# Rotations, turns, gates and norms spread between units, and MLA's four short projections interleaved with a longer one

## The chip, the cores and the metric

The kernel runs on one core of a Trainium2 chip, with inputs, weights and output in HBM. The metric is device time in microseconds of one execution. The engines of the core are TensorE (PE; its weight loads are PEld), VectorE (DVE), ScalarE (ACT), GpSimd (POOL) and SyncE (SP, which issues the DMAs); each runs its own program, and semaphores order them.

## The reference, cut to what matters

256 tokens of width 1024 in float32 go through two layers of a first block and two of a second.

```python
# first block, per layer (h = rms_norm(x))
cq, ckv, k_rope, mq, mk, mv, rq, rk, rv, rg, g_mla, g_moba, g_ret = split(h @ w_in)
q  = rms_norm(cq) @ w_q_up;  kv = rms_norm(ckv) @ w_kv_up        # MLA's short projections
o_mla  = causal_attention(q, [kv_nope, rope(k_rope)], v)          # 8 heads, rope on 32 of 96
o_moba = causal attention of partial_rope(mq), partial_rope(mk), mv   # 8 heads of 64
o_ret  = silu(rg) * group_norm(retention(rope(rq), rope(rk), rv))     # 4 heads, decay in place of softmax
merged = sum(sigmoid(g_i) * (o_i @ w_branch_i));  x = x + merged @ w_out
x = x + square(relu(rms_norm(x) @ w_mlp_up)) @ w_mlp_down
# second block, per layer (u = rms_norm(h))
gq, gk, gv, gg, ra_f, ra_b, aq, ak, av, gate_a, gate_b = split(u @ w_in)
branch_a = (rms_norm(gla(gq, gk, gv, decays)) * silu(gg)) @ w_o_gla
branch_b = gqa(axial_rope(rms_norm(aq)), axial_rope(rms_norm(ak)), av) @ w_o_attn   # 8 heads of 128
h = h + rms_norm((sigmoid(gate_a) * branch_a + sigmoid(gate_b) * branch_b) @ w_out)
# then a gated MLP and a gated embedding
```

## The kernel before, in words

Every weight matrix is cut into chunks of at most 512 columns, and a chunk into *units* of two blocks of 128 rows. `Plan` lists the 600 units in the order in which every engine goes through them (`units_first`: 140 in each first layer, `units_second`: 160 in each second one; numbers below count within a layer). For a unit SyncE loads 128x1024 floats into one of four `raw` slots; ScalarE copies them to `hi`, rounded (L1015); VectorE takes `lo` = `raw` - `hi` (L1396; GpSimd for some of the MLP's units); TensorE makes twelve products (L556): two row tiles, two blocks, and hi x hi, lo x hi, hi x lo. The short `kv_up` chunks have one block, six products. A chunk accumulates in one of two pairs of PSUM banks, `acc`; pairs alternate from chunk to chunk, and a chunk's first product waits until the earlier chunk of its pair is drained (`pair0_drained`, `pair1_drained`).

`Stream.to(n)` and `Stream.on(n)` go to unit n of the layer, or n units on. Everything else is written by hand between such calls, and each engine's own list of calls sets where in its queue a piece stands. ScalarE is three units ahead with `hi`, VectorE two with `lo`, and both read out a finished chunk one unit later (`after` and `read_out`, EVAC = 1). So VectorE's queue has the low part of unit v + 3 ahead of the read-out of a chunk that ended at unit v.

The order in a first layer: `w_in` chunks in units 0 to 11 (latents, MQ, MK), `q_up` in 12 and 13, `kv_up` in 14 and 15, MV 16 to 19, RQ with RK 20 to 23, RV 24 to 27, RG (`silu`) 28 to 31, the gates 32 to 55, then the branches. VectorE rotates MoBA's rows at 13 and MLA's q at 17 (`rope_heads`, six instructions of L1526 to L1531). At 19 TensorE transposes ("turns") MLA's q and k into the four `mix` banks (L523); ScalarE copies q to `qT`, VectorE k to `kT` (L1414); TensorE waits for these (`emptied`) and starts the heads. A head is: scores on TensorE (L585, L627), shift on VectorE (L1546, L1549), exponential on ScalarE (L1104), a turn (L604), a copy to `probT` by ScalarE (L1029), the context (L616). `MLA_UNITS`, `RET_UNITS` and `MOBA_UNITS` say how many units stand in each step. In a step with scores these stand between the turn and the context that needs its copy; in MoBA only even steps have them. Retention follows MLA and MoBA follows retention, each with turns and copies at its opening. Group norm and gating of retention's output (`retention_out`, five steps) lie beside MoBA's heads.

In a second layer (`second_layer`) the four heads of gated linear attention stand at units 30 to 41; beside them VectorE makes the squares and rotations of the grouped attention's q and k (`head_squares`, `head_rope`). At 46 these are turned, after `rows_ready`; from 48 on come its eight heads, two units each, with exponentials at L1275 and copies to `attnT` at L1029, waited for at L824. The gate chunks are units 40 to 55, read out with Sigmoid at L1123. Where ScalarE changes between functions of different tables, it runs an ACT_TABLE_LOAD first.

Of the kernel before, what the change touches and what calls it, by code (L numbers as in the profile page):

```python
# [129 lines left out]

def units_first(ln):
# [16 lines left out]
    return (woven(p[0], p[1]) + straight(p[2], *q_up, *kv_up, *p[3:])  # L148
# [4 lines left out]
def units_second(ln):  # L153
# [30 lines left out]
    'bank0_filled'        : [103, 0, 0],  # L184
    'bank1_filled'        : [106, 0, 0],
    'bank2_filled'        : [106, 0, 0],
    'bank3_filled'        : [86, 0, 0],
    'bank0_drained'       : [103, 0, 0],
    'bank1_drained'       : [106, 0, 0],
    'bank2_drained'       : [106, 0, 0],  # L190
    'bank3_drained'       : [86, 0, 0],
    'pair0_drained'       : [73, 0, 0],
    'pair1_drained'       : [73, 0, 0],
# [3 lines left out]
    'rows_ready'          : [66, 0, 0],  # L197
# [8 lines left out]
    'gates_ready'         : [2, 0, 0],  # L206
    'glu_ready'           : [18, 0, 0],
# [26 lines left out]
class Plan:  # L234


    def __init__(self):
# [262 lines left out]
def tensor_program(nc, pe, n, L):  # L500
# [120 lines left out]
    def softmax_heads(tag, heads, q, k, v, units):  # L621
        blocks = {(1, 0): 0, (1, 1): P, (0, 0): TOK}
        for h in range(heads + 2):
# [5 lines left out]
            if h >= 2:  # L629
                emptied((tag, "t", h - 2))  # L630
# [12 lines left out]
    def first_layer():  # L643
# [9 lines left out]
        s.to(19)  # L653
# [10 lines left out]
        pe.wait_ge(*n.next("rows_ready"))  # L664
        for w, col in (("q", RQ), ("k", RK)):
            turn(("ret", w, 0), lambda t, k: L.proj[:, t, col + k * P:col + (k + 1) * P], (0, 1))
        turn_half("mla", 0, y_tile)
        emptied(("ret", "q", 0)); emptied(("ret", "k", 0))
        for h in range(RET_H + 1):
# [5 lines left out]
            s.on(RET_UNITS[h])  # L675
            if h:
# [4 lines left out]
        for w, col in (("q", MQ), ("k", MK)):  # L681
            for j in range(2):
                turn(("moba", w, j), lambda t, k: L.proj[:, t, col + k * P:col + (k + 1) * P], (2 * j, 2 * j + 1))
# [6 lines left out]
        s.to(50)  # L690
        pe.wait_ge(*n.next("rows_ready", 2))
        turn_half("moba", 0, y_tile)
        s.to(55)
# [26 lines left out]
    def second_layer():  # L720
# [90 lines left out]
        for h in range(AQ_H + 2):  # L811
            if h < AQ_H:
                kv = h // (AQ_H // AKV_H)
                fill(("gqa", "s", h), lambda b: [nc.tensor.matmul(L.mix[:, b, t * TOK:(t + 1) * TOK], L.qT[:, h, t * P:(t + 1) * P],  # L814
                                                                 L.kT[:, kv, :], **f32) for t in range(NT)], (0, 1, 2))
            if h >= 2:
# [20 lines left out]
            s.on(2 if 1 <= h <= 8 else 0)  # L837
# [164 lines left out]
Q_SCALE, VAR_G, ROOT_G = 232, 96, 136  # L1002
# [3 lines left out]
def scalar_program(nc, act, n, L, io):  # L1006
# [144 lines left out]
    def sigmoids(*cols):  # L1151

        for c in L.plan.chunks:
            if c.ln == ln and c.name == "gate" and any(g <= c.to < g + D for g in cols):
                act.wait_ge(*n.at(f"pair{c.pair}_drained", c.turn + 1))
        for g in cols:
            last = nc.scalar.activation(L.proj[:, :, g:g + D], L.proj[:, :, g:g + D], ACT.Sigmoid)
        last.then_inc(*n.up("gates_ready"))
# [16 lines left out]
    def first_layer():  # L1175
# [7 lines left out]
        s.to(19)  # L1183
        for j in range(4):
            empty(("mla", "q", j), L.qT[0:QK_D, 2 * j:2 * j + 2, :], 2 * TOK, QK_D)
# [941 lines left out]
```

## Time and profile before

| | |
|---|---|
| median of 3 runs | 1988.53 us (1987.27 to 1989.32) |
| the profiled execution's own time | 1988.42 us |
| its span, first to last instruction | 1986.3 us |
| TensorE products | 96% of the span |
| VectorE; ScalarE; GpSimd | 63%; 50%; 6% |
| mean granted TensorE clock | 0.988 |
| `lo` (L1396), x552 | 1226 ns each |
| `hi` (L1015), x600 | 1060 ns each |

The profile is of one execution. An engine is busy from the start to the end of an instruction; idle time is told with what ended it. TensorE's clock is the granted share of its full speed of 2.4 GHz. A product of 512 columns is recorded with some 390 ns, but the next begins earlier, since they are pipelined.

### The profile page before, as it was taken

The numbers are of one execution on the slowest core, as the hardware profiler recorded it, in microseconds if no ns is written. First come the engines' busy times: TensorE is split into PE (matmuls) and PEld (weight loads), VectorE is DVE, ScalarE is ACT, GpSimd is POOL, SyncE is SP. The second block draws the span as 40 slices with busy tenths as digits, with TensorE's granted clock in tenths as the row PEclk, the third lists the DMA queues.
The fourth block names the chain that finished last, engine by engine and source line by source line (L and its number), as shares of the span: only waits on it lengthen the run. The fifth ranks groups of instructions, "written<-read, shape, count | busy, mean of one in ns | idle before, by whom it ended". The sixth has DMA issues, their size and how long they took to land.

```text
span 1986.3 us, 25019 instructions
## 1 busy us (share of the span) xinstructions
PE 1906.1 (96%) x9121; PEld 1550.8 (78%) x9121; DVE 1254.4 (63%) x2095; ACT 995.4 (50%) x1516; POOL 127.9 (6%) x52
## 2 busy tenths in 40 slices
PE   7899999999999999999999999999989999999997
PEld 6777788888777788877777887888767777878885
DVE  6756674546756574545768657666675695676656
ACT  4445554444445554444653746545456347464544
POOL 0000008300000007500000000000000000000000
PEclk9999999999999999999999999999989999999999
DMA  6444555565534556555543444656544344455562
GB/s 225 136 125 130 167 172 180 183 186 180 159 106 123 176 162 195 169 174 155 189 131 122 128 159 148 196 160 205 171 123 162 122 128 128 149 176 184 169 204 93
DMA packets 167500, 315.33 MB, mean 159 GB/s; under 512 B 12282, under 2 KB 20172, under 8 KB 167252
## 3 DMA queue, kind: packets, MB, share of 16 engines
q1 hardware_dynamic: 166784, 312.01, 50.6%
q8 instruction: 74, 1.21, 0.2%
q10 hardware_dynamic: 596, 1.73, 0.2%
q14 instruction: 46, 0.38, 0.1%
HBM read 312.65 MB, written 1.05 MB: 158 GB/s over the span
## 4 chain that ended last, share of the span: by engine, by line
PE 85%; DVE 8%; ACT 4%; issue 2%; DMA 0%; ACTq 0%; DVEq 0%
PE acc L556 73%; PE mix L523 4%; DVE lo L1396 2%; PE mix L616 2%; ACT hi L1015 1%; PE mix L824 1%; PE mix L795 1%; PE mix L585 1%; PE mix L814 1%; PE mix L782 1%; PE mix L604 1%; ACT junk L1090 0%; DVE kT L1414 0%; PE mix L754 0%; DVE x L1496 0%
## 5 line engine op out<-in xcount | busy, mean ns | idle before, releaser
L1015 ACT ACTIVATE hi<-raw 128x1024 fp32r<-128x1024 f32 x600 | 633.2, 1060 | 599.6 <-PE acc L556 546.9
L1396 DVE TENSOR_TENSOR lo<-raw,hi 128x1024 fp32r<-128x1024 f32 x552 | 665.6, 1226 | 217.4 <-ACT hi L1015 201.7
L556 PE MATMUL acc<-hi,xTh 128*128 128x512 f32 (+3 forms) x1760 | 696.6, 396 | 24.2 <-DVE lo L1396 14.6
L556 PE MATMUL acc<-hi,xTl 128*128 128x512 f32 (+3 forms) x1760 | 680.1, 386 | 0.0
L556 PE MATMUL acc<-lo,xTh 128*128 128x512 f32 (+3 forms) x1760 | 679.3, 386 | 0.0
L556 PEld LDWEIGHTS acc<-hi,xTh 128*128 128x128 f32 x1760 | 335.0, 190 | 106.6 <-issue 39.8
L556 PEld LDWEIGHTS acc<-hi,xTl 128*128 128x128 f32 x1760 | 334.3, 190 | 66.8
L556 PEld LDWEIGHTS acc<-lo,xTh 128*128 128x128 f32 x1760 | 335.4, 191 | 59.8
L987 POOL TENSOR_TENSOR lo<-raw,hi 128x1024 fp32r<-128x1024 f32 x48 | 127.7, 2687 | 694.5 <-ACT hi L1015 694.5
L556 PE MATMUL acc<-hi,hTh 128*128 128x512 f32 x432 | 172.0, 398 | 0.3 <-DVE lo L1396 0.3
L556 PE MATMUL acc<-hi,hTl 128*128 128x512 f32 x432 | 171.2, 396 | 0.0
L556 PE MATMUL acc<-lo,hTh 128*128 128x512 f32 x432 | 171.2, 396 | 0.0
L1424 DVE TENSOR_TENSOR hTl<-mix,hTh 128x256 fp32r<-128x256 f32 x108 | 38.4, 418 | 119.1 <-ACT hTh L1037 119.1
L556 PEld LDWEIGHTS acc<-hi,hTh 128*128 128x128 f32 x432 | 81.4, 188 | 20.0 <-issue 0.7
L556 PEld LDWEIGHTS acc<-hi,hTl 128*128 128x128 f32 x432 | 81.4, 188 | 19.8
L556 PEld LDWEIGHTS acc<-lo,hTh 128*128 128x128 f32 x432 | 81.4, 188 | 19.3
L1037 ACT ACTIVATE hTh<-mix 128x256 fp32r<-128x256 f32 x108 | 32.9, 390 | 54.0 <-PE mix L523 54.0
L556 PE MATMUL acc<-hi,oTh 128*128 128x512 f32 (+1 forms) x136 | 54.5, 401 | 5.1 <-DVE y L1582 5.1
L556 PE MATMUL acc<-lo,oTh 128*128 128x512 f32 (+1 forms) x136 | 53.6, 394 | 0.0
L556 PE MATMUL acc<-hi,oTl 128*128 128x512 f32 (+1 forms) x136 | 53.5, 393 | 0.0
L1104 ACT ACTIVATE prob<-prob,small 128x256 f32<-128x256 f32 x64 | 28.7, 449 | 49.3 <-DVE small L1549 49.3
L523 PE MATMUL mix<-const,y 128*128 128x128 f32 (+1 forms) x360 | 48.2, 279 | 0.0
(222 smaller groups left out, 1614.3 us busy)
## 6 DMA issues: line engine op xcount, KB each, us to landing
raw<-in_w_in SPq DMA_DIRECT2D x200, 512.0 KB, 3.8
raw<-in_w_ffn_in SPq DMA_DIRECT2D x80, 512.0 KB, 4.3
raw<-in_w_mlp_up SPq DMA_DIRECT2D x64, 512.0 KB, 3.8
raw<-in_w_mlp_down SPq DMA_DIRECT2D x64, 512.0 KB, 4.5
raw<-in_w_ffn_out SPq DMA_DIRECT2D x44, 512.0 KB, 4.3
raw<-in_w_out SPq DMA_DIRECT2D x32, 512.0 KB, 4.1
raw<-in_w_o_gla SPq DMA_DIRECT2D x16, 512.0 KB, 3.7
raw<-in_w_o_attn SPq DMA_DIRECT2D x16, 512.0 KB, 3.7
```

Source lines behind the costliest of these rows:

```text
L523: yield nc.tensor.transpose(L.mix[0:width, b, i * TOK + t * P:i * TOK + (t + 1) * P], rows(t, k), L.ident)
L556: last = nc.tensor.matmul(out, a[:, t * P:(t + 1) * P], w[:, slot, part, 0:c.n], start=(k == 0 and a is ah and w is L.hi), stop=(k == c.k_ ...
L585: yield nc.tensor.matmul(L.mix[:, b, c:c + w], q[:, a:a + P], k[:, 0:w], start=True, stop=True)
L604: yield nc.tensor.transpose(L.mix[:, b, i * P:(i + 1) * P], L.prob[:, h % 2, i * P:(i + 1) * P], L.ident)
L616: last = nc.tensor.matmul(L.mix[:, b, (t * per + i) * dv:(t * per + i + 1) * dv], L.probT[:, h % 2, c:c + P], v(kt, h), start=(kt == 0), s ...
L782: last = nc.tensor.matmul(L.mix[:, b, m * GLA_V:(m + 1) * GLA_V], L.ks[r, d, c // 2, h * P:(h + 1) * P], gv(r, c // 2), **f32)
L987: nc.gpsimd.tensor_tensor(L.lo[:, slot], L.raw[:, slot], L.hi[:, slot].bitcast(F32), ALU.subtract).then_inc(*n.up("low_by_pool"))
L1015: nc.scalar.activation(L.hi[:, slot], L.raw[:, slot], ACT.Copy).then_inc(*n.up("hi_ready"))
L1037: last = nc.scalar.activation(dst, L.mix[:, b, i * TOK:(i + 1) * TOK], ACT.Copy if gain is None else ACT.Identity, scale=scale)
L1104: last = nc.scalar.activation(p, p, ACT.Exp, bias=L.small[:, SHIFT + 2 * s + 1 - t:SHIFT + 2 * s + 2 - t], scale=scale, accum_out=L.small[ ...
L1396: v.tensor_tensor(L.lo[:, slot], L.raw[:, slot], L.hi[:, slot].bitcast(F32), ALU.subtract).then_inc(*n.up("low_by_dve"))
L1424: last = v.tensor_tensor(lo, src, hi.bitcast(F32), ALU.subtract)
```

## The change

Short projections: `between` puts one unit of MV behind each of the four, and a chunk's pair is now the other one than that of the unit before. Turns of MLA, retention and MoBA: one unit (`BEHIND_TURNS`) between the turns and the wait for their copies; retention's turns go ahead of MLA's last context, MLA's output is turned inside retention, three of MoBA's four turns stand ahead of retention's last context; steps have other numbers of units. VectorE's MoBA rotation moves to head 1 of MLA, `retention_out` a step later and its last step to unit 54. RG is drained by Identity, and one Silu in place does the gate at 51; the sigmoids stand apart. In the second layers low parts go between the halves of the rotations, the group norm's roots move into the heads (`gla_roots`), gates are drained by Identity with two late sigmoids, and the last heads have a unit ahead of each context.

```diff
+def between(short, c):
+
+    return [(a, 0) if i == 0 else (c, j) for j, a in enumerate(short) for i in range(2)]
...
-    return (woven(p[0], p[1]) + straight(p[2], *q_up, *kv_up, *p[3:])
+    return (woven(p[0], p[1]) + straight(p[2]) + between([*q_up, *kv_up], p[3]) + straight(*p[4:])
...
-                c.pair = len(self.chunks) % 2
+                c.pair = 1 - self.unit[u - 1][0].pair if u else 0
...
-MLA_UNITS = [2, 2, 2, 1, 2, 2, 1, 2, 1, 0]
-RET_UNITS = [0, 1, 1, 1, 1]
-MOBA_UNITS = [2, 1, 1, 1, 2, 1, 1, 1, 1, 0]
+MLA_START, BEHIND_TURNS = 21, 1
+MLA_UNITS = [1, 2, 2, 1, 2, 1, 1, 2, 1, 0]
+RET_UNITS = [0, 1, 1, 1, 0]
+MOBA_UNITS = [1, 1, 1, 1, 2, 1, 1, 1, 1, 0]
```

TensorE, first layers (`softmax_heads` and `first_layer`):

```diff
             if h >= 2:
+                if h == heads + 1 and ahead_of_last:
+                    ahead_of_last()
                 emptied((tag, "t", h - 2))
...
-        s.to(19)
+        s.to(MLA_START)
         pe.wait_ge(*n.next("rows_ready"))
...
+        s.on(BEHIND_TURNS)
         for j in range(4):
             emptied(("mla", "q", j)); emptied(("mla", "k", j))
+        def turn_ret():
+            pe.wait_ge(*n.next("rows_ready"))
+            for w, col in (("q", RQ), ("k", RK)):
+                turn(("ret", w, 0), lambda t, k: L.proj[:, t, col + k * P:col + (k + 1) * P], (0, 1), among=(0, 1, 2))
+
         softmax_heads("mla", MLA_H, lambda h: L.qT[0:QK_D, h, :], lambda h: L.kT[0:QK_D, h, :],
-                      lambda t, h: L.vm[:, t, h, :], MLA_UNITS)
...
+                      lambda t, h: L.vm[:, t, h, :], MLA_UNITS, turn_ret)
+
+        s.on(BEHIND_TURNS)
         emptied(("ret", "q", 0)); emptied(("ret", "k", 0))
...
             s.on(RET_UNITS[h])
+            if h == 2:
+                pe.wait_ge(*n.next("rows_ready"))
+                turn_half("mla", 0, y_tile, (0, 1, 2))
+            if h == RET_H:
+                for w, col, j in (("q", MQ, 0), ("q", MQ, 1), ("k", MK, 0)):
+                    turn(("moba", w, j), lambda t, k: L.proj[:, t, col + k * P:col + (k + 1) * P], (2 * j, 2 * j + 1), among=(0, 1, 2))
...
+        turn(("moba", "k", 1), lambda t, k: L.proj[:, t, MK + k * P:MK + (k + 1) * P], (2, 3), among=(0, 1, 2))
+        s.on(BEHIND_TURNS)
```

TensorE, second layers:

```diff
+            if h >= AQ_H:
+                s.on(1)
             if h >= 2:
...
-            s.on(2 if 1 <= h <= 8 else 0)
+            s.on(2 if 1 <= h < AQ_H else h == AQ_H)
```

ScalarE:

```diff
-        if c.name == "gate":
+        if c.name == "gate" or c.name == "silu" and ln < LAYERS:
...
-                                            ACT.Identity if ln < LAYERS and c.to < G_MOBA else ACT.Sigmoid if ln >= LAYERS or c.to < G_RET else ACT.Identity,
+                                            ACT.Sigmoid if c.name == "gate" and ln < LAYERS and G_MOBA <= c.to < G_RET else ACT.Identity,
...
+    def silu_of_retention():
+
+        c = next(c for c in L.plan.chunks if c.ln == ln and c.name == "silu")
+        act.wait_ge(*n.at(f"pair{c.pair}_drained", c.turn + 1))
+        nc.scalar.activation(L.proj[:, :, RG:RG + COLS], L.proj[:, :, RG:RG + COLS], ACT.Silu).then_inc(*n.up("silu_ready"))
...
-        s.to(50)
+        s.to(51)
+        silu_of_retention()
+        s.to(52)
         split_half("moba", 0)
-        sigmoids(G_MLA, G_RET)
+        s.to(53)
+        sigmoids(G_MLA)
         s.to(55)
+        sigmoids(G_RET)
+        s.to(57)
         split_half("ret", 0)
...
+            if h == AQ_H - 1:
+                s.on(1)
+                sigmoids(at2(G_A))
+                s.on(1)
...
+        s.to(67)
+        sigmoids(at2(G_B))
```

VectorE, first layers:

```diff
-        s.to(13)
-        rope_heads(proj[:, :, MQ:MV].rearrange("p t (h d) -> p t h d", d=MOBA_D), 2 * MOBA_H, MOBA_R // 2, "moba")
-        s.to(17)
+        s.to(18)
         rope_heads(y[:, :, 0:MLA_H * QK_D].rearrange("p t (h d) -> p t h d", d=QK_D)[:, :, :, NOPE:], MLA_H, ROPE // 2, "mla")
+        s.to(20)
         tell("rows_ready")
...
+            if h == 1:
+                rope_heads(proj[:, :, MQ:MV].rearrange("p t (h d) -> p t h d", d=MOBA_D), 2 * MOBA_H, MOBA_R // 2, "moba")
+            elif h == 3:
                 rope_heads(proj[:, :, RQ:RV].rearrange("p t (h d) -> p t h d", d=RET_K), 2 * RET_H, RET_K // 2, "ret")
-
+                tell("rows_ready")
...
-        softmax_heads("moba", MOBA_H, MOBA_D ** -0.5, 0, MOBA_UNITS, lambda h: retention_out(h) if h < 5 else None)
+        softmax_heads("moba", MOBA_H, MOBA_D ** -0.5, 0, MOBA_UNITS, lambda h: retention_out(h - 1) if 1 <= h < 5 else None)
...
+        s.to(54)
+        retention_out(4)
```

VectorE, second layers:

```diff
-            elif h == 2:
-                for t in range(NT):
-                    head_rope(0, 4, t)
-            elif h == 3:
-                head_squares(4, 8)
-                for t in range(NT):
-                    head_rope(4, 8, t)
-            s.on(3)
+            if h in (1, 3):
+                head_squares(2 * h - 2, 2 * h + 2)
+            s.on(1)
+            if h >= 2:
+                head_rope(4 * h - 8, 4 * h - 4, 0)
+            s.on(1)
+            if h >= 2:
+                head_rope(4 * h - 8, 4 * h - 4, 1)
+            s.on(1)
         head_squares(8, 10)
         s.on(1)
         head_roots()
         s.on(1)
-        for t in range(NT):
-            head_rope(8, 10, t)
+        scale_keys()
+        head_rope(8, 10, 0)
+        s.on(1)
+        head_rope(8, 10, 1)
         tell("params_free")
         tell("tmp_free")
         tell("rows_ready")
...
-            if h < 2:
-                gla_out(h)
...
+            if h == 0:
+                gla_roots()
+            elif h < AQ_H:
+                s.on(1)
+                if h <= 2:
+                    gla_out(h - 1)
+                s.on(1)
```

`gla_roots` holds the group norm's instructions that stood at `s.to(45)`, unchanged.

## Rows read from the trace of the kernel before

**Rows 1.** The page, busy time of each engine.

```profile
PE 1906.1 (96%) x9121; PEld 1550.8 (78%) x9121; DVE 1254.4 (63%) x2095; ACT 995.4 (50%) x1516; POOL 127.9 (6%) x52
```

**Rows 2.** Waits of TensorE (in total, times, longest, us).

```profile
PE acc L556 <- DVE lo L1396: 14.9, 22, 2.0
...
PE mix L616 <- ACT probT L1029: 9.2, 14, 1.1
...
PE mix L824 <- ACT attnT L1029: 7.1, 6, 2.2
```

**Rows 3.** Windows: us, busy by engine (instructions), PE clock, DMA.

```profile
73.27:76.68 3.41, 3.41 (x10) 2.64 (x9) 2.44 (x7) 1.93 (x5) 0.00 (x0) 0.50 0.18 17
...
440.00:460.00 20.00, 20.00 (x87) 16.10 (x86) 8.90 (x8) 7.43 (x7) 0.00 (x0) 1.00 0.64 189
...
588.68:592.09 3.41, 3.41 (x10) 2.63 (x9) 1.94 (x3) 0.00 (x0) 0.00 (x0) 0.50 0.13 15
```

**Rows 4.** Timeline of TensorE, first layers: start, us; idle before in brackets.

```profile
46.62 0.39 PE L556 MATMUL acc<-hi,oTh 128*128 128x512 f32 x1
...
53.36 0.51 PE L556 MATMUL acc<-hi,oTh 128*128 128x512 f32 x1 [2.37 <-DVE y L1582]
...
55.41 0.50 PE L556 MATMUL acc<-hi,oTh 128*128 128x512 f32 x1 [0.37 <-DVE y L1582]
...
58.24 0.50 PE L556 MATMUL acc<-hi,xTh 128*128 128x512 f32 x1 [1.17 <-DVE vm L1582]
...
72.03 0.89 PE L585 MATMUL mix<-kT,qT 96*128 96x256 f32 x4 [1.83 <-DVE kT L1414]
...
126.03 0.88 PE L616 MATMUL mix<-vm,probT 128*128 128x64 f32 x6 [1.12 <-ACT probT L1029]
...
130.64 0.88 PE L616 MATMUL mix<-vm,probT 128*128 128x64 f32 x6 [0.58 <-ACT probT L1029]
...
132.60 1.09 PE L523 MATMUL mix<-const,proj 128*128 128x128 f32 x8 [1.08 <-DVEq L1388]
...
151.24 1.97 PE L523 MATMUL mix<-const,proj 128*128 128x128 f32 x16 [0.79 <-DVE y L1746]
...
154.65 0.92 PE L627 MATMUL mix<-kT,qT 64*128 64x256 f32 x8 [1.45 <-DVE kT L1414]
...
587.35 0.92 PE L673 MATMUL mix<-qT,kT 64*128 64x256 f32 x8 [2.04 <-DVE oTl L1424]
```

**Rows 5.** Timeline of VectorE at the short projections.

```profile
48.37 0.42 DVE L1526 TENSOR_TENSOR tmp<-proj,const 128x256 f32<-128x256 f32 x1
...
56.53 0.87 DVE L1582 TENSOR_SCALAR km<-acc,small 128x256 f32<-128x256 f32 x2
...
57.32 0.87 DVE L1582 TENSOR_SCALAR vm<-acc,small 128x256 f32<-128x256 f32 x2
...
61.05 0.42 DVE L1526 TENSOR_TENSOR tmp<-y,const 128x256 f32<-128x256 f32 x1
```

**Rows 6.** ScalarE by line and form (xcount, busy us, mean ns, idle before).

```profile
L1157 ACT ACTIVATE proj<-proj 128x2048 f32<-128x2048 f32 x4 | 7.4, 1906 | 0.0
```

**Rows 7.** Window of a second layer, columns as in rows 3.

```profile
1066.12:1092.18 26.06, 24.07 (x113) 18.22 (x113) 24.32 (x80) 9.54 (x14) 0.00 (x0) 1.00 0.45 140
```

**Rows 8.** Timeline of all engines, the same second layer.

```profile
1078.48 0.47 PE L556 MATMUL acc<-hi,xTh 128*128 128x512 f32 x1 [1.99 <-DVE lo L1396]
...
1091.52 0.28 DVE L1531 TENSOR_TENSOR proj<-proj,tmp 128x128 f32<-128x128 f32 x1
...
1092.18 2.35 PE L523 MATMUL mix<-const,proj 128*128 128x128 f32 x20
...
1093.36 0.17 DVE L1951 TENSOR_SCALAR small<-small 128x8 f32<-128x8 f32 x1
...
1106.74 1.28 ACT L1123 ACT_TABLE_LOAD   x1
...
1110.79 1.56 PE L824 MATMUL mix<-proj,attnT 128*128 128x128 f32 x6 [2.16 <-ACT attnT L1029]
```

More of the change, by code:

```diff
@@ L196 @@
     'scaled_rows'         : [4, 0, 0],
-    'rows_ready'          : [66, 0, 0],
+    'rows_ready'          : [68, 0, 0],
     'ple_rows'            : [8, 0, 0],
@@ L619, in context, with softmax_heads @@
             last.then_inc(*n.up(f"bank{b}_filled"))
-    def softmax_heads(tag, heads, q, k, v, units):
+    def softmax_heads(tag, heads, q, k, v, units, ahead_of_last=None):
         blocks = {(1, 0): 0, (1, 1): P, (0, 0): TOK}
@@ L689, in first_layer @@
                       lambda t, h: L.proj[:, t, MV + h * MOBA_D:MV + (h + 1) * MOBA_D], MOBA_UNITS)
-        s.to(50)
-        pe.wait_ge(*n.next("rows_ready", 2))
+        s.to(52)
+        pe.wait_ge(*n.next("rows_ready"))
         turn_half("moba", 0, y_tile)
-        s.to(55)
+        s.to(57)
+        pe.wait_ge(*n.next("rows_ready"))
         turn_half("ret", 0, lambda t, k: L.y[:, t, COLS + k * P:COLS + (k + 1) * P])
@@ L1149, in embedded, with sigmoids @@
         nc.scalar.activation(L.embed[:, :, c.to:c.to + COLS], pair(c), ACT.Copy).then_inc(*n.up(f"pair{c.pair}_drained"))
-    def sigmoids(*cols):
+    def sigmoids(g):
         for c in L.plan.chunks:
-            if c.ln == ln and c.name == "gate" and any(g <= c.to < g + D for g in cols):
+            if c.ln == ln and c.name == "gate" and g <= c.to < g + D:
                 act.wait_ge(*n.at(f"pair{c.pair}_drained", c.turn + 1))
-        for g in cols:
-            last = nc.scalar.activation(L.proj[:, :, g:g + D], L.proj[:, :, g:g + D], ACT.Sigmoid)
-        last.then_inc(*n.up("gates_ready"))
+        nc.scalar.activation(L.proj[:, :, g:g + D], L.proj[:, :, g:g + D], ACT.Sigmoid).then_inc(*n.up("gates_ready"))
+    def silu_of_retention():
+        c = next(c for c in L.plan.chunks if c.ln == ln and c.name == "silu")
+        act.wait_ge(*n.at(f"pair{c.pair}_drained", c.turn + 1))
+        nc.scalar.activation(L.proj[:, :, RG:RG + COLS], L.proj[:, :, RG:RG + COLS], ACT.Silu).then_inc(*n.up("silu_ready"))
     def hidden(c):
@@ L1585, in read_out @@
     def read_out(c):
-        if c.name in ("gate", "plain", "ple") or c.name == "normed" and (c.weight == "w_out_2" or c.to):
+        if c.name in ("gate", "plain", "ple") or c.name == "silu" and ln < LAYERS or c.name == "normed" and (c.weight == "w_out_2" or c.to):
             return
@@ L1600, in read_out @@
         elif c.name.startswith("branch"):
-            if c.name == "branch_mla" and c.to == 0:
+            if c.name != "branch_moba" and c.to == 0:
                 dve.wait_ge(*n.next("gates_ready"))
@@ L1604, in read_out @@
                  "branch_gla": at2(G_A), "branch_attn": at2(G_B)}[c.name] + c.to
-            if c.name not in ("branch_mla", "branch_ret"):
+            if c.name == "branch_moba":
                 gate = L.plan.chunk(ln, "gate", g)
@@ L1677, in retention_out @@
         elif step == 4:
+            dve.wait_ge(*n.next("silu_ready"))
             link(v.tensor_tensor(o, o, proj[:, :, RG:RG + COLS], ALU.mult))
@@ L1829, in head_rope, with gla_roots @@
         rope(r[:, :, :, 0, :], r[:, :, :, 1, :], c, sn, [end - first, 2, A_D // 4], L.tmp, c_b=c_b, s_b=s_b)
+    def gla_roots():
+        dve.wait_ge(*n.next("squared", NT * GLA_H))
+        link(v.tensor_scalar(col(VAR_G, 8), col(VAR_G, 8), NORM_EPS, None, ALU.add))
+        inverse_root(VAR_G, ROOT_G, 8)
+        b, use = L.banks.get((ln, "gla", "o", GLA_H - 1))
+        dve.wait_ge(*n.at(f"bank{b}_drained", use + 1))
     def gla_out(g):
@@ L1948, in second_layer @@
         tell("rows_ready")
-        s.to(45)
-        dve.wait_ge(*n.next("squared", NT * GLA_H))
-        link(v.tensor_scalar(col(VAR_G, 8), col(VAR_G, 8), NORM_EPS, None, ALU.add))
-        inverse_root(VAR_G, ROOT_G, 8)
-        b, use = L.banks.get((ln, "gla", "o", GLA_H - 1))
-        dve.wait_ge(*n.at(f"bank{b}_drained", use + 1))
         s.to(46)
@@ L1982, in second_layer @@
                 split_half("attn", 0)
-            s.on(2 if 1 <= h <= 8 else 0)
+            if h == 0:
+                gla_roots()
+            elif h < AQ_H:
+                s.on(1)
+                if h <= 2:
+                    gla_out(h - 1)
+                s.on(1)
+            elif h == AQ_H:
+                s.on(1)
         s.to(66)
```

69 lines of the change are left out of this document (37 added, 32 removed).

## The prediction

> **What bounds the kernel now.** I read the page first: TensorE is busy 1906.1 of 1986.3 us [rows 1], so no edit to another engine is worth more than the 80.2 us in which TensorE stands idle, plus what its clock loses. The waits of TensorE come next [rows 2]: the reader is to see that they are many and short, 22 on VectorE's low parts, 14 on a transposed probability block, and none longer than 2.5 us but two at the start of the kernel and of a block. Then the windows by stage [rows 3]: a plain stretch makes 87 matmuls in 20 us, 0.23 us each, 2.76 us for a unit of twelve, with VectorE and ScalarE under half busy. So in the long stages nothing can be won, and the change leaves them alone. The same view has stretches of 3.41 us at a granted clock of 0.50, that is the 1.2 GHz level in place of 2.4, each worth 1.7 us. I find five of them in the stages touched: at 73.3, 506.8, 588.7, 1110.9 and 1643.4; two stand in the rows. Each began within 1.4 us after a TensorE wait of 1.8 to 2.4 us. But of nine such waits in these stages (53.4, 72.0, 505.7, 524.4, 587.4, 1078.5, 1110.8, 1610.9, 1643.3) four had no such stretch behind them. Last, TensorE's timeline gives the place and size of each wait [rows 4].
>
> **The change, part by part.** The sum is made against the profiled execution, 1988.42 us, which is its span of 1986.3 and 2.1 around it; the median of the runs, 1988.53, is the same to 0.1 us.
>
> *Short projections, first layers.* Now the four follow one another, and each needs the accumulator pair of the last but one. The MoBA rotation (six VectorE instructions of 0.42 us, 2.4 in all) and the low parts stand before the read-outs, and TensorE waits 2.37, 0.37 and 1.17 us in layer 0 [rows 4], 2.37 and 0.10 in layer 1. After: all four use one pair, with a unit of MV between. TensorE, from the first matmul at 46.62: q_up 2.8, MV 2.75, second q_up (256 columns, an estimate of half a unit) 1.45, MV 2.75, kv_up (six matmuls) 1.4, MV 2.8, kv_up 1.4, MV 2.8, which is 64.8. VectorE: the read-outs of the two q_up come in time (51.0 against 52.2; 55.6 against 56.4). Then the low part of unit 19 can't begin before unit 15 is done (56.4) and ScalarE's copy of 1.06 has followed, so it ends at 58.9; first kv_up read-out 0.87 + 0.79 [rows 5], 60.6, just in time; the q rotation, moved in front of `s.to(20)`, 2.36 (0.42 each, at 61.05 and five more), 63.0; two low parts, 65.3; second kv_up read-out 1.66, 67.0. Unit 20 needs that pair and stands ready at 64.8: a new wait of 2.15 us. So the wait that takes the place of the old ones is VectorE's second kv_up read-out. The unit added behind the turns covers the copies to kT: 1.83 goes. Layer 0: 2.37 + 0.37 + 1.17 + 1.83 - 2.15 = 3.6, with the slow stretch at 73.3 (1.7) 5.3. Layer 1: 2.37 + 0.10 + 1.83 - 2.15 = 2.15, with that at 506.8 3.85. The DMAs of the short weights are issued one unit apart in place of back to back, in the same queue and number; I cost them at nothing, because no TensorE wait here ends on a transfer. MoBA's rotation goes to head 1 of MLA: there VectorE has two units, 5.5 us, for two low parts, a shift, a read-out and the 2.4 us, 7.1 us in all, but its low parts run two units ahead, so 1.6 us late is inside the slack of one unit. Uncovered it would cost that 1.6 us a layer.
>
> *Heads' end, retention, MoBA's opening.* At the end of MLA TensorE waits 1.12 (a table load and a sigmoid read-out stand ahead of the block's copy), 0.58 (no scores cover the last head's copy) and 1.08 (`rows_ready`, told only after the heads) [rows 4]. After, the silu chunk is drained by Identity with no load, and 1.12 becomes the 0.58 that all heads without scores have: 0.54 won. Retention's turns stand ahead of the last head's context and cover 0.58; `rows_ready` is told at head 3, 1.08 won. At MoBA's opening 0.79 and 1.45 go: bank 3 isn't used for turns any more, and a unit stands behind them. Layer 1 alone also has 2.04 for the low parts of MLA's output [rows 4], and the slow stretch at 588.7 behind it; the turn moves a stage later, with a unit behind. 0.54 + 0.58 + 1.08 + 0.79 + 1.45 = 4.44 per layer; 2.04 + 1.7 more in layer 1. The added wait on `rows_ready` before MLA's half has retention's contexts queued behind it, but three units lie since its signal. The five waits of 0.58 in MoBA stay, since odd heads still have no scores ahead.
>
> *Silu.* The trace has no Silu. Its bounds are the Copy of the same tile, 1.06 us, and the Sigmoid of a tile twice as wide, 1.91, plus one table load, 1.28, or none [rows 6, 8]; I take 1.06 with a load ahead of it and one more at the sigmoids behind it. With these, and the two sigmoids of 1.91 put apart, ScalarE's high part of unit 56 ends 13.9 us after unit 50 began and VectorE's low part at 15.1, where TensorE wants it at 17.3: 2.2 us to spare, 1.3 with the longer instruction. So nothing is on the path at either end; uncovered, the load and the instruction would cost 2.3 us a layer. VectorE loses two multiplications per layer, off the path.
>
> *Second layers.* VectorE is the bound from 1066.12 to 1092.18: 24.32 us busy of 26.06 [rows 7], the rest being the gaps between dependent instructions. TensorE waits 1.99 at 1078.48, then reaches the turns of gqa at 1092.18, right when the last rotation is done (1091.52 + 0.28, signals 0.3) [rows 8]. The change puts a low part between the halves of each rotation, and the wait of 1.99 goes. But VectorE's work before `rows_ready` is not less: it gains one low part (unit 46's), 1.15 us, and the group norm's roots, moved back, stood behind `rows_ready` anyway. So it ends at 1093.2, and TensorE, now earlier, waits there about 2.9 us and 1.1 before, at unit 43. The turns come 1.05 us later than before: a loss. In the heads, the 2.16 at 1110.79 is ScalarE's chain to the first attnT copy: table load 1.28, read-out, copy [rows 8]. The load goes; but the roots (twelve instructions, 0.2 apart from 1093.36 on, 2.43 in all [rows 8]) stand between the two shifts where gla_out(0) stood with four of 0.42, 1.67: 1.28 - 0.76 = 0.5 is won, with the slow stretch of 1.7 behind it. Of the six waits on attnT [rows 2] the other four are (7.1 - 2 x 2.16) / 4 = 0.69 each, two a layer, at the last heads, and are covered by units: 1.38. Two more switches between kinds of matmul cost 0.12 each. Layer: 0.5 + 1.7 + 1.38 - 1.05 - 0.24 = 2.3. Deferred sigmoids are two instructions of 1.91 on ScalarE, which copies high parts three units ahead (5.9 us of slack against 3.2): nothing.
>
> The Trainium skill ("ScalarE: Activation LUTs", section "What ACT_TABLE_LOAD costs") gives 1283 ns for the load and a drain of some 1380 ns more. Here the load at 1106.74 takes 1.28 us and the activation behind it begins at 1108.04, so this trace shows no drain. By the page the sum would be 1.4 us larger in each second layer, 2.8 in all.
>
> *Sum.* 5.3 + 4.4 in layer 0, 3.85 + 4.4 + 3.7 in layer 1, 2 x 2.3: 26.3 us with no new slow stretch. New waits of 2.15 (twice) and 2.9 (twice) are of the size of which five in nine were followed by one; I count two, 3.4 us. Won: 22.9. 1988.4 - 22.9 = 1965.5.
>
> **Rivals.**
> *Every cover holds.* If VectorE catches up at unit 20 and before gqa, neither new wait appears: 26.3 + 2 x 2.15 + 2 x (1.05 + 1.99) = 36.7, 1951.7. For it: VectorE is idle half the time elsewhere. Against: the chain above has no slack from 58.9 on. Chance 0.15.
> *The clock.* Slow stretches behind all four new waits and both of those at attnT that stay (1.6 us): 26.3 - 6 x 1.7 = 16.1, 1972.3. For it: five in nine. Chance 0.17.
> *The covers do less than they say.* The waits at the ends of stages are VectorE's and ScalarE's backlog, not the delay of one copy, and come back behind the next unit: then 2 x 4.44 + 2.04 are not won, 15.4 less 3.4, 1976.4. For it: 151.24 and 154.65 stand in a row. Against: what ends most of them is one copy that was issued as soon as its turn was done [rows 4]. Chance 0.10.
> *Slower: the heads fall behind.* MLA's heads get 13 units in place of 15, MoBA's 10 in place of 11. If a head's chain (shift, exponential, transpose, copy) no longer fits behind a single unit, TensorE waits at each head, at 1.12 us as at 126.03: 32 heads, 35.8 us, 1965.5 + 35.8 = 2001.3. It decides from 0.72 us a head. Against: single-unit heads with scores ahead show no wait at all, all 14 of [rows 2] are at heads without. Chance 0.05.
> The forecast itself has 0.53, with 1959 to 1971.
>
> **How the numbers follow.** The range reaches from between the first rival and the forecast to the third: 1953 to 1977. About 0.2 % is what this measurement can tell from no change. Faster than that 0.92, same 0.03, slower 0.05.
>
> **What would show it.** Right: no TensorE wait at the kv_up units, one of 2 us before unit 20 that ends on VectorE's vm; no wait at the first scores of MLA, retention and MoBA; one of 2 to 3 us at gqa's turns that ends on VectorE's rotation; attnT's first wait near 1.6; no ACT_TABLE_LOAD at the read-out line of the gates. Wrong: waits of 0.6 to 1.1 us at heads that have scores ahead, or more than two slow stretches in these stages.

## The result, and the profile after

The changed kernel takes 1964.83 us (median of 4 runs, 1963.9 to 1965.03) where the kernel before, on the same chip, takes 1987.99 (4 runs, 1987.27 to 1989.32): ratio 0.9877, 95% interval 0.9865 to 0.9889. The forecast was 1965.5 in a range of 1953 to 1977, and "faster" had a chance of 0.92. The profiled execution took 1965.03 us, span 1963.1, which is 23.2 less than before.

Busy time by engine on the page, to be held against [rows 1]: TensorE's busy time fell by 3.4 us, its idle time by 19.8.

```profile
PE 1902.7 (97%) x9121; PEld 1550.2 (79%) x9121; DVE 1251.3 (64%) x2091; ACT 987.7 (50%) x1510; POOL 127.9 (7%) x52
```

TensorE's waits (in total, times, longest), to be held against [rows 2]. Low parts fell from 14.9 to 11.4 us, transposed blocks from 14 to 12, attnT from six to two. Two lines have other waits under them than before: vm has the second kv_up read-out in both first layers (before, one wait of 1.17), and the turns' wait on VectorE's signal (DVEq) is now at gqa's turns, 2.5 each, where before it was at retention's, 1.1 each.

```profile
PE acc L563 <- DVE lo L1437: 11.4, 19, 1.6
...
PE mix L623 <- ACT probT L1049: 7.0, 12, 0.6
PE mix L530 <- DVEq L1429: 4.9, 2, 2.5
...
PE acc L563 <- DVE vm L1623: 3.9, 2, 2.0
PE mix L844 <- ACT attnT L1049: 2.7, 2, 1.3
```

TensorE's timeline (start, us; idle before in brackets), answering to [rows 4] and to the rows of TensorE in [rows 8]. A row without brackets began without a wait: so do the first scores of MLA (L592), retention (L685) and MoBA (L634), where before 1.83, 2.04 (layer 1) and 1.45 stood.

```profile
67.61 0.50 PE L563 MATMUL acc<-hi,xTh 128*128 128x512 f32 x1 [1.95 <-DVE vm L1623]
...
78.35 0.82 PE L592 MATMUL mix<-kT,qT 96*128 96x256 f32 x4
...
124.68 0.88 PE L623 MATMUL mix<-vm,probT 128*128 128x64 f32 x6 [0.58 <-ACT probT L1049]
...
132.94 0.92 PE L685 MATMUL mix<-qT,kT 64*128 64x256 f32 x8
...
151.36 0.92 PE L634 MATMUL mix<-kT,qT 64*128 64x256 f32 x8
...
510.20 0.50 PE L563 MATMUL acc<-hi,xTh 128*128 128x512 f32 x1 [1.95 <-DVE vm L1623]
...
1091.78 1.16 PE L844 MATMUL mix<-proj,attnT 128*128 128x128 f32 x8 [1.34 <-ACT attnT L1049]
...
1604.35 0.89 PE L530 MATMUL mix<-const,proj 128*128 128x128 f32 x6 [2.45 <-DVEq L1429]
```

Windows (columns as in [rows 3]) of four of the ten stretches at a granted clock of 0.50, the 1.2 GHz level: the first and last are the only ones in stages that the change touches, the other two stand in layer 2's opening (its first units, up to gated linear attention), which it doesn't touch.

```profile
69.07:72.49 3.41, 3.41 (x11) 2.62 (x10) 1.25 (x2) 0.00 (x0) 0.00 (x0) 0.50 0.61 181
929.23:936.06 6.83, 5.21 (x14) 4.17 (x15) 5.75 (x10) 2.12 (x2) 0.00 (x0) 0.50 0.77 250
963.37:966.78 3.41, 3.41 (x10) 2.64 (x9) 3.19 (x3) 0.91 (x1) 0.00 (x0) 0.50 0.32 124
1605.07:1608.48 3.41, 3.41 (x18) 3.32 (x17) 0.83 (x2) 2.84 (x5) 0.00 (x0) 0.50 0.62 184
```

**Where the time went.** I took the start of the same unit's first matmul in both traces, at both ends of each stage touched. In layer 0 the unit before the short projections starts 0.69 us later than before, the second unit of MLA's branch 9.21 earlier: 9.9 won. Likewise layer 1, from 9.09 to 22.57 earlier: 13.5; layer 2, from 19.05 to 22.54: 3.5; layer 3, from 21.17 to 23.07: 1.9. That is 28.8 in all. Outside, 5.6 were lost: 0.7 in the first 44 us, 3.5 in the opening of layer 2, 1.4 in that of layer 3. Where times of a stage are compared below, they are taken in the same way.

### The profile page after: what moved, and what is told of

Its sections match the earlier page's. It is cut to its first block, busy times and chain, and to the rows that moved or that the text cites. A ratio compares the mean times of both kernels' runs of the same rounds, so it can differ in the third digit from the quotient of the medians.

```text
span 1963.1 us, 25017 instructions
## 1 busy us (share of the span) xinstructions
PE 1902.7 (97%) x9121; PEld 1550.2 (79%) x9121; DVE 1251.3 (64%) x2091; ACT 987.7 (50%) x1510; POOL 127.9 (7%) x52
## 3 DMA queue, kind: packets, MB, share of 16 engines
HBM read 312.65 MB, written 1.05 MB: 160 GB/s over the span
## 4 chain that ended last, share of the span: by engine, by line
PE 85%; DVE 8%; ACT 4%; issue 2%; DMA 1%; ACTq 0%; DVEq 0%
PE acc L563 73%; PE mix L530 4%; DVE lo L1437 2%; PE mix L623 2%; ACT hi L1035 1%; PE mix L844 1%; PE mix L611 1%; PE mix L592 1%; PE mix L832 1%; PE mix L813 1%; DVE x L1537 0%; PE mix L800 0%; DVE proj L1623 0%; PE mix L772 0%; ACT junk L1110 0%
## 5 line engine op out<-in xcount | busy, mean ns | idle before, releaser
L563 PE MATMUL acc<-hi,xTh 128*128 128x512 f32 (+3 forms) x1760 | 698.4, 397 | 23.3 <-DVE lo L1437 11.4
L563 PEld LDWEIGHTS acc<-hi,hTl 128*128 128x128 f32 x432 | 81.4, 188 | 19.8
```

What stands on the lines that cost most here:

```text
L563: last = nc.tensor.matmul(out, a[:, t * P:(t + 1) * P], w[:, slot, part, 0:c.n], start=(k == 0 and a is ah and w is L.hi), stop=(k == c.k_ ...
```

## The experiments

Every kernel below was timed in 5 rounds beside the kernel before: e1 to e4 on one chip, e5 to e8 on another, e9 to e11 on a third. The kernel before had 1992.3 us on the first, 1988.6 and 1988.3 on the others, so ratios are compared, and above all the traces. A trace is of one execution, and its time can lie some us off the median.

**Read-out ahead (e1).** Is the new wait of 1.95 VectorE's backlog?

```diff
         s.to(18)
-        rope_heads(y[...], MLA_H, ROPE // 2, "mla")
+        rope_heads(y[...], MLA_H, ROPE // 2, "mla", (0,))   # first two of six instructions
+        s.to(19)
+        read_out(L.plan.chunk(ln, "kv_up", 4), now=True)
         s.to(20)
+        rope_heads(y[...], MLA_H, ROPE // 2, "mla", (1,))
         tell("rows_ready")
```

> The changed kernel (1964.8 us) with one edit to VectorE's order in the first layers: the second kv_up read-out stands ahead of unit 21's low part, and of the q rotation only the first two of six instructions stand ahead of it. Theory: the wait of 1.95 us before unit 20 is VectorE's backlog (rotation 2.4 + two low parts 2.4 + read-out 1.7 behind the first read-out), so it goes in both layers, and with it the stretch at half clock behind the first: 2 x 1.95 + 1.7 = 5.6 us, 1959.2. Rival: the rotation is now told later, and TensorE waits the same time before the turns of unit 21 in place of unit 20: 1963 to 1965. Second rival, on the clock: the stretch at half clock comes in this place anyway; then 1961.

Measured: 1956.9 us, ratio 0.9828 (0.9809 to 0.9847). VectorE's timeline in the changed kernel and in this one: in the first, the rotation and two low parts (63.63 to 66.0) stand between the two km/vm read-outs, in the second, two of the rotation's instructions and one low part. From the end of one read-out to the end of the next it is 6.4 us in the first and 3.6 in the second.

```profile
60.34 0.87 DVE L1623 TENSOR_SCALAR vm<-acc,small 128x256 f32<-128x256 f32 x2
61.24 0.42 DVE L1567 TENSOR_TENSOR tmp<-y,const 128x256 f32<-128x256 f32 x1
...
63.63 2.36 DVE L1437 TENSOR_TENSOR lo<-raw,hi 128x1024 fp32r<-128x1024 f32 x2
...
66.69 0.87 DVE L1623 TENSOR_SCALAR vm<-acc,small 128x256 f32<-128x256 f32 x2
```

```profile
59.66 0.87 DVE L1626 TENSOR_SCALAR vm<-acc,small 128x256 f32<-128x256 f32 x2
60.56 0.43 DVE L1568 TENSOR_TENSOR tmp<-y,const 128x256 f32<-128x256 f32 x1
...
61.35 1.23 DVE L1437 TENSOR_TENSOR lo<-raw,hi 128x1024 fp32r<-128x1024 f32 x1
...
63.28 0.87 DVE L1626 TENSOR_SCALAR vm<-acc,small 128x256 f32<-128x256 f32 x2
64.18 1.23 DVE L1437 TENSOR_TENSOR lo<-raw,hi 128x1024 fp32r<-128x1024 f32 x1
```

No TensorE wait over 0.15 us is left between unit 12 and MLA's heads, not at the turns either, so the first rival is out. The stretch at half clock after unit 20 went with the wait; behind the turns of both second layers there was one. The profiled execution, with a long stretch in layer 2's opening, is the slowest of the four (1959.5; the others 1953.8 to 1957.0). In layer 1, where neither kernel has a stretch, the stage takes 2.25 us less, for a wait of 1.95.

**Keys turned a unit later (e2).** Is the wait at gqa's turns for the keys alone?

```diff
+        tell("rows_ready")                      # VectorE: q's rows, ahead of the keys' squares
         head_squares(8, 10)
...
         # TensorE, behind the four turns of q
+        s.on(1)
+        pe.wait_ge(*n.next("rows_ready"))
         turn(("gqa", "k", 0), ...)
```

> The changed kernel with the turns of gqa's q and k parted in the second layers: q's rows are told ready before the squares of the key heads (which q's turns don't need), and the key turn stands one unit later with a wait of its own. Theory: the waits of 2.48 and 2.45 us at gqa's turns are for the keys' part of VectorE's work alone, and unit 46 covers it: 4.9 us less, 0.24 for two more switches, and 1.7 for the stretch at half clock behind the wait at 1604: 1958.5. Rival: VectorE is the bound of the whole stretch up to there, so TensorE, no longer held, runs into it one or two units later, at the key turn or a low part: 1963 to 1965.

Measured: 1956.2 us, ratio 0.9823 (0.9806 to 0.9839). In its trace q's turns and the keys' stand apart and neither waits, and no stretch at half clock is left in the second layers' heads. VectorE's backlog was real but had a unit to spare, once only the keys hung on it. The time is lower than the 1958.5 expected, in part by luck: neither wait of 1.95 at unit 20 has a stretch behind it in this trace. Layer 0, where nothing was edited, is 1.6 us shorter for that.

```profile
1069.34 1.91 PE L530 MATMUL mix<-const,proj 128*128 128x128 f32 x16
1073.84 0.60 PE L530 MATMUL mix<-const,proj 128*128 128x128 f32 x4
```

**Roots behind the second shift (e3).**

```diff
-            if h == 0:
-                gla_roots()
-            elif h < AQ_H:
+            if 1 <= h < AQ_H:
+                if h == 1:
+                    gla_roots()
                 s.on(1)
```

> The changed kernel with the roots of the group norm (eleven VectorE instructions, 2.4 us) behind the second head's shift in place of between the first two. Theory: they delay the second exponential, and with it ScalarE's high part and the first attnT copy: exponential 2.0 us earlier, copy 1.05 earlier (then the high part of unit 52, which wants unit 49 used, stands ahead of it), so the wait of 1.34 falls to 0.3 in both layers: 1962.7. Rival: the copy is late for the gate's read-out and two high parts, not for the shift, and nothing changes: 1964.8.

Measured: 1964.7 us, ratio 0.9868 (0.9851 to 0.9884). The time is the rival's, but not for its reason, and the theory's 1962.7 was missed. The copy did come earlier, and the context at 1090.56 (it was 1091.78) doesn't wait. But the second turn behind it, of gla's rows, takes a bank that the third exponential still reads, and waits 1.42. (The roots are twelve instructions in the trace, not eleven.) The timelines of TensorE and ScalarE show it:

```profile
1090.56 1.14 PE L844 MATMUL mix<-proj,attnT 128*128 128x128 f32 x8
1091.54 0.60 PE L530 MATMUL mix<-const,y 128*128 128x128 f32 x4
1093.55 0.66 PE L530 MATMUL mix<-const,y 128*128 128x128 f32 x4 [1.42 <-ACT attn L1307]
```

```profile
1089.89 0.60 ACT L1049 ACTIVATE attnT<-mix 128x512 f32<-128x512 f32 x1 [0.50 <-PE mix L860]
1092.30 0.56 ACT L1307 ACTIVATE attn<-mix,small 128x256 f32<-128x256 f32 x1 [1.81 <-DVE small L2021]
```

**One after another (e4).** The order of the short projections undone, the rest kept (VectorE's rotation of q is back at unit 17, since the turns come two units earlier).

```diff
-    ... straight(p[2]) + between([*q_up, *kv_up], p[3]) + straight(*p[4:])
+    ... straight(p[2], *q_up, *kv_up, *p[3:])
-MLA_START, BEHIND_TURNS = 21, 1
+MLA_START, BEHIND_TURNS = 19, 1            # and MLA_UNITS = [2, 2, 2, 1, 2, 2, 1, 2, 1, 0]
```

> The changed kernel with the four short projections of the first layers one after another again, as in the kernel before; MoBA's rotation stays at MLA's head 1 and every cover stays. Theory A: what held TensorE there was the rotation ahead of the read-outs, not the order; then 2.37 us at the first kv_up stays away (0.4 and 1.2 us are left in layer 0, about none in layer 1), the new wait of 1.95 us before unit 20 isn't there, nor the stretch at half clock behind it: 1964.8 - 3.9 - 1.7 + 1.6 = 1960.8. Theory B: the interleaving is what removes the waits; then 2.4 + 0.4 + 1.2 us come back in layer 0 and 2.4 in layer 1 in place of 2 x 1.95: 1967.

Measured: 1962.9 us (1958.7 to 1963.3), ratio 0.9859 (0.9841 to 0.9878). TensorE's timeline has theory A's waits: the 2.37 at the first kv_up stays away without the interleaving, and 0.38 and 1.17 are left (both in layer 1 too, which I hadn't expected).

```profile
54.24 0.50 PE L563 MATMUL acc<-hi,oTh 128*128 128x512 f32 x1 [0.38 <-DVE y L1623]
57.07 0.50 PE L563 MATMUL acc<-hi,xTh 128*128 128x512 f32 x1 [1.17 <-DVE vm L1623]
```

So in the changed kernel the interleaving trades these for 1.95, and by itself is worth nothing that these ratios can tell. In layer 1, where neither trace has a stretch, the stage takes the same time to 0.1 us.

**MoBA's rotation back (e7)** at unit 13, the interleaving kept.

```diff
+        s.to(13)
+        rope_heads(proj[:, :, MQ:MV]..., "moba")
         s.to(18)
...
-            if h == 1:
-                rope_heads(proj[:, :, MQ:MV]..., "moba")
```

> The changed kernel with MoBA's rotation (2.4 us of VectorE) back at unit 13, where it stood before, and the interleaved short projections kept. Theory A: the rotation is what made the read-outs late; the first q_up read-out then ends at 54.1 in place of 51.7, TensorE waits 1.9 us at unit 14 in each first layer beside the 1.95 before unit 20, and the time is 1968.6. Theory B: with a unit between the projections VectorE's idle 2.2 us at 53 and 57.5 take it up: no new wait, and the time is 1964.8.

Measured: 1968.9 us (1966.9 to 1969.7), ratio 0.9896 (0.9878 to 0.9914). The wait at unit 14 is there in both layers, 1.05 us each in place of the 1.9 expected: VectorE's idle time takes up the rest (1.28 us stood idle ahead of its low part at 54.27 in the changed kernel, none there in this one). Theory A with half its size; the ratio alone would not separate it from the changed kernel.

```profile
53.58 0.39 PE L563 MATMUL acc<-hi,oTh 128*128 128x256 f32 x1 [1.05 <-DVE y L1623]
```

**No unit behind the turns (e5)** (`BEHIND_TURNS = 0`, the first entries of MLA_UNITS, RET_UNITS and MOBA_UNITS one larger).

> The changed kernel (1964.8 us) without the unit behind the turns at the openings of MLA, retention and MoBA; the unit goes behind the first scores instead. Theory: the unit covers the copies of the turned tiles, so without it the waits of the kernel before come back, 1.83 us at MLA's first scores and 1.45 at MoBA's in each first layer (retention's turns stand ahead of a context and a unit's worth of work, and cost nothing): 6.6 us, 1971.4, and up to 1.7 more for each stretch at half clock behind the two of 1.83. Rival: the copies were late for VectorE's backlog, which the change removed elsewhere; then nothing comes back, 1965.

Measured: 1975.0 us (1971.8 to 1976.0), ratio 0.9923 (0.9908 to 0.9937). The waits are back at their old size, 1.90 and 1.45 in each first layer, only 0.21 at retention's first scores, and a stretch at half clock stands behind one of the 1.90 (at 523.0). The stages take 3.7 us more in layer 0 and 5.4 in layer 1, the latter with that stretch. So these two covers do what they say; the median is above the 1971.4 of the theory, the profiled execution (1971.8, the fastest of five) is not.

```profile
77.56 0.89 PE L592 MATMUL mix<-kT,qT 96*128 96x256 f32 x4 [1.90 <-DVE kT L1455]
```

**Second layers undone (e6)** (their code of the kernel before, under the changed first layers).

> The changed kernel's first layers with the second layers of the kernel before (rotations whole, all roots and the gate's sigmoids where they were, no unit in the heads' last two steps). By the waits of both traces the second layers' part is worth 1.99 + 2.16 + 2 x 0.69 less 2.48 + 1.34, 1.7 us a layer, and the clock's stretch at 1110.9 in one of them: 1964.8 + 3.4 + 1.7 = 1969.9. By the prediction's terms without the clock it is 0.6 a layer: 1966 to 1967.7. If all the gain is in the first layers: 1964.8.

Measured: 1969.6 us (1969.1 to 1970.0), ratio 0.9898 (0.9883 to 0.9913). It is near the number from the waits (1969.9). In layer 2 they stand again at 1057.24 (2.00), 1089.52 (2.16), and twice 0.69, in layer 3 likewise; another, of 0.61 in layer 2 and 0.92 in layer 3, is at gla's turns, in the place where "roots behind" had its own. That the number fits is in part chance: in this trace the edited stages take 5.6 and 2.7 us more than in the changed kernel, with a stretch of 6.83 at 1090.66 that I hadn't counted, and 1.6 us come back in the first layers, where no stretch stands behind unit 20.

**Three edits together (e8)**: read-out ahead, keys behind, and roots behind with gla's turn moved behind a unit.

```diff
             if h == 2:
+                s.on(1)
                 pe.wait_ge(*n.next("rows_ready"))
                 turn_half("gla", 0, y_tile, (0, 1, 2))     # and so on ScalarE and VectorE
```

> Three edits together: the second kv_up read-out ahead (e1), gqa's keys turned a unit later (e2), and, with the roots behind the second shift (e3), the turn of gla's first half one unit later, since in e3 the wait of 1.33 on attnT became one of 1.42 at the second of those turns, which takes the bank that the third exponential still reads. Theory: the waits are independent, so 2 x (1.95 + 2.46 + 1.33) = 11.5 us of TensorE's idle time go, 0.5 comes for switches, and no stretch at half clock is left in the stages touched (two in the changed kernel, 3.4): 1950.4. Rival: VectorE's work before gqa's heads holds the third shift as well, and the wait moves once more, to 1.3 us somewhere behind: 1953.

Measured: 1948.2 us (1946.5 to 1949.7), ratio 0.9791 (0.9775 to 0.9806). No wait over 0.15 us but the 0.58s, and no stretch at half clock, is left in the stages touched. The theory, that the waits are independent, had 1950.4; its rival had 1953.

**The unit ahead of the context (e9)**, for the 0.58s themselves; with all edits (e10); and the changed kernel once more beside them (e11).

```diff
+def late(tag, heads, h):
+    return h >= 2 and (h >= heads or tag == "moba" and h % 2 == 1)
...
+                if late(tag, heads, h):
+                    s.on(units[h])
                 emptied((tag, "t", h - 2))
                 context(tag, h - 2, v, MLA_V, blocks, 4)
-            s.on(units[h])
+            if not late(tag, heads, h):
+                s.on(units[h])                              # VectorE likewise; MOBA_UNITS ends in 1
```

> The changed kernel with one edit to the softmax heads of the first layers: at a head that brings no scores (odd heads of MoBA and the last steps of both) the unit stands ahead of the context in place of behind it, and the last step of MoBA gets a unit. Theory: the twelve waits of 0.58 us (one in MLA, five in MoBA, in each layer) are the uncovered ScalarE copy of the transposed block, which the unit now covers: 7.0 us, 1957.8. Rival: the transposed block of the next head then comes right behind the context and the next scores cover it no longer, or VectorE, which waits for the group's output ahead of its low parts, falls behind: waits of the same size at the even heads, 1965.

> All edits together: read-out ahead, keys turned later, roots and gla's turn later (these three gave 1948.2), and the unit ahead of the context at heads without scores. If the last is independent of the others: 1948.2 - 7.0 = 1941.2. If it isn't: 1948.

> The changed kernel as it is, on the chip and in the call of the two kernels above, so that they can be held against it: 1964.8, and in its trace the waits of 1.95, 1.95, 2.48, 2.45, 1.34 and 1.33 us again. The stretches at half clock are looked at: if a wait of a certain place and size brings one with certainty, they stand at 69.1 and 1605.1 again and not at 511 and 1074.

Measured: 1952.5, 1934.3 and 1965.6 us; ratios 0.9822 (0.9807 to 0.9836), 0.9735 (0.9720 to 0.9750) and 0.9889 (0.9873 to 0.9906). The edit alone brings 13.1 us against the changed kernel beside it, where twelve waits of 0.58 make 7.0 and 1957.8 was expected. TensorE's timeline at one head, in the changed kernel:

```profile
162.11 0.49 PE L611 MATMUL mix<-const,prob 128*128 128x128 f32 x3
163.18 0.75 PEld L623 LDWEIGHTS mix<-proj,probT 128*128 128x128 f32 x6 [0.82 <-ACT probT L1049]
163.18 0.88 PE L623 MATMUL mix<-proj,probT 128*128 128x64 f32 x6 [0.58 <-ACT probT L1049]
```

and in the one with the unit first, where a unit follows the transposes at 160.03 and the context comes at 162.87:

```profile
159.78 0.49 PE L615 MATMUL mix<-const,prob 128*128 128x128 f32 x3
...
162.87 0.78 PE L627 MATMUL mix<-proj,probT 128*128 128x64 f32 x6
163.48 0.50 PE L615 MATMUL mix<-const,prob 128*128 128x128 f32 x3
```

From transposes to what follows it was 1.07 us, and is 0.25; the context took 0.69 to the next instruction's start and takes 0.61. So the wait of 0.58 cost 0.9: 0.24 more is the end of the last matmul before it, which otherwise overlaps the next, and 0.08 the start of the first one behind it. Its weight load (PEld above) waited 0.82 and starts with it, so I read the 0.08 as weights that were not loaded ahead; no run tests that by itself. Twelve such are 10.8. The traces show it directly: over the two first layers' stages the kernel with the unit first takes 10.6 us less, with one stretch at half clock in each of the two kernels. Beyond these it wins 3.5 in layer 2's opening, which the edit doesn't touch (below), and loses 1.7 to a stretch at gqa's turns, so the 13.1 is not the edit's own worth.

With all edits TensorE is never idle in the touched part of a first layer, as the windows show (us, then TensorE's busy time):

```profile
45.00:215.00 170.00, 170.00 (x902) 142.48 (x901) 117.70 (x242) 93.79 (x167) 0.00 (x0) 1.00 0.52 150
488.00:660.00 172.00, 172.00 (x904) 143.72 (x903) 118.42 (x241) 94.86 (x169) 0.00 (x0) 1.00 0.53 153
```

This kernel, 1934.3 us, beats both: 31.3 less than the changed one beside it. The expected 1941.2 was 6.9 too high. Over the first layers' stages its trace gains 10.5 us on that of the three edits, not the 7.0 of the sum, and its opening of layer 2 is one of the short ones (below).

## Why the prediction was right

The number was right within 0.7 us, but that closeness is luck, two errors of opposite sign: 28.8 us were won in the stages touched, where 26.3 less 3.4 were counted, and 5.6 were lost outside, where I had counted nothing. The mechanisms of most terms held.

*Short projections.* Right in mechanism, place and size: no wait at the kv_up units, 1.95 before unit 20 where 2.15 was forecast, on VectorE's vm, in both layers. VectorE's chain ran as worked out, 0.6 to 0.7 later throughout (last read-out done at 67.6 for 67.0), and TensorE was ready 0.9 later (65.7 for 64.8). What I did not see is that the interleaving is not needed for this gain: with the rotation's move alone the stage takes the same time (e4). Whether an order like e1's would take away the waits that e4 still has, no run shows.

*MoBA's rotation in MLA's head 1.* Right: no wait in the heads behind it, and none at any head that has scores ahead, so the rival "the heads fall behind" is out too.

*Heads' end, retention, openings.* Right in each: 1.12 became 0.58, the last 0.58, 1.08, 2.04, 0.79 and 1.45 are gone, the five 0.58s stay, and without the covers of MLA's and MoBA's first scores those waits come back at their size (e5). The rival that the waits are a backlog is out: in the changed kernel's trace none comes back behind the next unit.

*Silu.* ScalarE's timeline: a load and the cost of the Copy, as taken, off the path. The sign "no ACT_TABLE_LOAD at the read-out line of the gates" holds in the second layers; each first layer still has one there (203.50 and 644.47), at the gate chunks that are read out with Sigmoid, as the change has it.

```profile
195.35 1.28 ACT L1182 ACT_TABLE_LOAD   x1
196.65 1.06 ACT L1182 ACTIVATE proj<-proj 128x1024 f32<-128x1024 f32 x1
```

The Trainium skill ("ScalarE: Activation LUTs", "What ACT_TABLE_LOAD costs") gives some 1380 ns of drain beside the load's 1283. The activation here begins 0.02 us after the load, so this trace again shows none.

*Second layers.* The turns came late, as said: layer 2 enters the stage 19.05 us earlier than before, so with no delay they would be at 1092.18 - 19.05 = 1073.1, and they are at 1074.07: 0.9 late for a forecast of 1.05. The wait there is 2.48 for "about 2.9", that at attnT 1.34 for 1.6, the 0.69s are gone. The further wait of 1.1 at unit 43 did not come: with low parts between the halves of the rotations these came in time, and all the lateness met at one place. The term is mis-sized: 1.8 and 1.9 a layer without the clock, where mine makes 0.6 (2.3 less 1.7). The largest part lies at the last two heads, worth 1.9 in layer 2 where I had 1.38 less 0.24 for the switches; the wait at attnT fell by 0.8 for 0.5.

*The price of a wait.* This is what most terms had too small. I took a wait at the number in its bracket; one of 0.58 costs 0.9 (e9), and the one of 1.95 cost 2.25 (e1, layer 1). The two covers' waits of e5 cost less beyond their brackets: 3.7 in layer 0 where the brackets, with 0.21 at retention, make 3.56. In the change itself, the brackets that went less the one that came, with the stretches, make 8.2 in layer 0 and 12.2 in layer 1, where 9.9 and 13.5 were won: 1.7 and 1.3 more, for a net of seven waits each. So the price beyond the bracket was 0.1 to 0.3, and for waits other than these it is an estimate.

*The clock.* I counted two new stretches in the touched stages and there were two, at a wait of 1.95 and at one of 2.45. Over all traces that have them, the 16 waits of 1.9 to 2.0 at unit 20 had a stretch behind them 6 times, the 16 of 2.45 at gqa's turns 13 times: 19 of 32, near my five in nine. That this kernel had just two is a count near its mean, no more. The repeated kernel had them in the same two places, other kernels in others, so a wait's size doesn't settle it. Nor do they look independent of one another: of the eight traces with this wait at layer 2's turns, the three that had no stretch behind it are the three that had one at 986 to 989, late in that layer's opening; the five others had none there. Why, no run shows. The rival "the clock" asked for six, one behind each new wait and each at attnT; two came. "Every cover holds" did not come true either; the three edits together (e8) made it so, with the wait at attnT gone as well: 1948.2 where it had 1951.7.

*The step that failed.* "In the long stages nothing can be won, and the change leaves them alone" is false for the second layers' openings: they lost 3.5 and 1.4 us with not an instruction changed there. In layer 2 the long stretch at half clock stands 2.1 us ahead of unit 12 in place of 3.6 and two more follow; layer 3's opening has one more as well (at 1434.4). The other step that failed is the price of a wait, above. The two nearly cancelled.

## What to carry to other kernels

Price a wait of TensorE by its bracket and 0.1 to 0.3 us more for the overlap that it breaks, and don't leave the small ones that repeat: here twelve of 0.58 were worth 10.6 us in the traces. A wait that ends on a busy engine is first asked what of that engine's queue it really needs; both of the change's new waits went by moving one read-out and one signal, without less work. When a wait is removed and the time stays, look one instruction further for the next wait on the same chain.

## What was not expected of the hardware

The stretches at half clock in work that no edit touched don't stay where they were. In layer 2's opening the first one, of 6.8 us, stands at 929.2 in the changed kernel, 2.1 us before unit 12, which then waits 1.61; further ones follow at 963.4 and 987.3. In the kernel before it stands 3.6 us before the same unit, which waits 0.56, and none follows. In the eleven other traces: where it begins 3.4 to 3.9 us before unit 12 (three) the wait is 0.56 and none follows in that opening; where it begins 2.0 to 2.8 us before (six) the wait is 1.0 to 1.7 and one or two follow; where 4.3 or 4.4 us before (two), the stretch lasts 10.2 and one follows. From its first unit to unit 27 layer 2 takes 90.4 to 90.6 us in the first case and in the kernel before, 93.3 in the last, and 92.8 to 94.2 in the second; the changed kernel, with 94.3, is of that second case. That makes the 3.5 us lost in this opening, as much as a layer's part of one of the edits. The repeated kernel fell in the second case as its first profile did. Whether the place of the stretch is set by the waits before it, or by something outside the kernel, no run here settles. The unit's wait in rows of the repeated kernel and of the one with the unit first:

```profile
930.83 0.76 PE L563 MATMUL acc<-hi,xTh 128*128 128x512 f32 x1 [1.00 <-DVE lo L1437]
```

```profile
920.38 0.77 PE L567 MATMUL acc<-hi,xTh 128*128 128x512 f32 x1 [0.56 <-DVE lo L1444]
```
